# Four joints between the stages of a two-block transformer kernel: order of a projection loop, loads of a gate matrix and of expert rows, and the way sums are read back

## The chip, the cores and the metric

The kernel runs on one core of one Trainium2 chip. The metric is device time in microseconds (us). Before the change the median of 3 runs is 3617.73 us (3616.99 to 3620.08). The profiled execution took 3617.26 us; its span from the first to the last instruction is 3615.6 us, so 1.7 us lie around the span.

## The reference, cut to what matters

Two blocks are computed on 1024 tokens of width 1024, in float32. Each ends in a mixture of experts (32 experts, top 2; then 64 experts, top 8), computed in blocks of 128 slots.

```python
def first_block(x, ...):
    u = rms_norm(h, norm_mix_g)
    x_rnn, g_rnn, q_c, kv_c, k_pe, gate_logits = split(u @ w_in)
    ya = rg_lru(causal_conv(x_rnn)) * gelu(g_rnn)
    yb = mla(q_c, kv_c, k_pe, ...)          # low-rank q and kv, 16 heads, chunk-causal attention
    gates = sigmoid(gate_logits)            # [2, D]
    h = h + (gates[0] * ya + gates[1] * yb) @ w_out
    h = h + hier_moe(rms_norm(h), ...)      # 32 experts, top 2
    return h

def second_block(x, ...):
    mix = hybrid_mixer(h)                   # HGRN2 in four heads, and multiscale_pool, then w_out
    h = layer_norm(ALPHA * h + mix)
    h = layer_norm(ALPHA * h + moe_ffn(h))  # 64 experts, top 8, and one shared expert
    return h
```

In a mixture each token's row goes to its experts' blocks, `silu(x @ w_gate[e]) * (x @ w_up[e]) @ w_down[e]` is taken there, weighted, and added to the token's sum.

## The kernel before, in words

The kernel is a row of stages, each a function with its own block of instruction streams for TensorE (PE), VectorE (DVE), ScalarE (ACT), GpSimd (POOL) and SyncE (SP). A stage ends in a barrier of all engines: the next one starts when the last engine's stream is through. `T` = 8 token tiles of 128 rows, `C` = 8 chunks of 128 columns. In order:

- `begin`, `lru` (the recurrent branch, four blocks of 256 columns; POOL writes zeroes into the spare rows and into the second half of `token_sums`; at its end PE computes the low-rank projection of token tile 0, `low_rank`).
- `mla_project`: for each tile t, `turn_low(t)` transposes the normalized low-rank rows on PE (8 transposes, L662), `low_groups(t + 1)` multiplies the next tile's (L653), `up_groups(t)` multiplies the transposed rows, after DVE has taken them from PSUM (L804), with `w_uq` and `w_ukv` (L679), and between the two it calls `turn_heads(t - 1)` (L692). ACT takes each product; four PSUM banks turn in the order of the list `order`. The two matrices are loaded by SP at the stage's start (L629, L630).
- `attention`, whose SP stream loads the heads two pairs ahead.
- `merge`: the gates (L1133) with `w_gate` loaded in four quarters into two buffers (L1102), then `w_out`, and the rows for the experts are written to DRAM.
- `route1`: DVE picks the experts; SP asks for the weights of the first `W1` = 5 experts, three transfers of 1 MB each (L1626, L1631).
- `dispatch`: DVE computes masks, counts and slots; SP writes the weights by row (`dense`, L1454) into the same DRAM rows; the last DVE instruction (L1614) leaves the token of every slot in `G.slot_tok`. It is used for both mixtures. In the second one the shared expert's products stand in it too, until after the slots are known.
- `experts`: per block of 128 slots POOL gathers the rows (`gather`: index copy L1753, an addition L1756 that makes the index visible, indirect DMA L1757), PE transposes them (`turn_rows`, L1814), DVE copies them out (L1911 for the first, L1902), DVE copies the second half's expert weights into a staging buffer (`stage_gate_up`, L1888, one copy of 128x4096), PE multiplies (L1825, L1828, L1851, L1854), and POOL adds the result into `token_sums` in DRAM. A weight slot is loaded again when PE is through with it (the waits on `gu_ready`).
- `take_sums`: the sums lie in two halves of `token_sums`. SP reads the first half's eight row tiles (L1247); POOL adds the second half to each by an accumulating DMA when the first has landed (`add_second`, L1230); PE transposes (L1260), DVE copies (L1267).
- `hgrn`, `pooling` (SP asks for `w`, `w_pool`, `w_out` at L2273 to L2275; POOL clears the second half of the sums again with nine DMAs of 512 KB, L276), `mix_out`, `route2`, `dispatch`, `experts` for the second mixture (two of four weight slots are loaded before it, and SP asks for the other two at its start), `final_norm` (SP reads the sums, L2481, POOL adds the second half as above, ACT and DVE normalize each tile, SP writes it out).

```python
            for t in range(T):                    # mla_project, PE
                turn_low(t)
                if t + 1 < T:
                    low_groups(t + 1)
                up_groups(t)
            turn_heads(T - 1)
...
            v.wait_ge(x_turned, 1)                # experts, DVE, before its loop
            d.tensor_copy(x_t[:, 0], x_ps[:]).then_inc(x_ready, 1)
            stage_gate_up(0, 0)
            stage_gate_up(1, 1)
```

Of the kernel before, what the change touches and what calls it, by code (L numbers as in the profile page):

```python
# [18 lines left out]
F32 = mybir.dt.float32  # L19
# [6 lines left out]
P = 128  # L26
# [246 lines left out]
def zero_second(pool, sum_d, zero, zero_out):  # L273

    for t in range(T + 1):
        pool.dma_start(sum_d[S + P + t * P:S + P + (t + 1) * P, :], zero).then_inc(zero_out, 16)  # L276


def lru(nc, A, G, spare, sum_d, wcol, wgate, w_low, ps):
# [9 lines left out]
    with ph.ctx:  # L289
# [43 lines left out]
        def _(pool):  # L333
# [6 lines left out]
            zero_second(pool, sum_d, zero[:, 0:D], zero_out)  # L340
            pool.wait_ge(zero_out, 16 * (len(spare) + T + 1))
# [234 lines left out]
def mla_project(nc, A, G, qk_d, v_d, w_low, ps):  # L576
# [12 lines left out]
    with ph.ctx:  # L589
# [54 lines left out]
        def _(pe):  # L644
# [198 lines left out]
def attention(nc, A, G, qk_d, v_d, mask_d):  # L843
# [25 lines left out]
    with ph.ctx:  # L869
# [42 lines left out]
        def _(sp):  # L912
# [20 lines left out]
            for p in range(PAIRS - 2):  # L933
                reload(p)

# [125 lines left out]
def merge(nc, A, G, rows_d, sum_d, logits):  # L1061
# [5 lines left out]
    COL = 2 * D + Q_LORA + KV_LORA + ROPE + D  # L1067
    HC = C // 2
    with ph.ctx:
        w_gate = ph.sb("w_gate", [P, 2, C, D // 4])  # L1070
# [17 lines left out]
        (wg0, wg1, wo_in, x_in, g_ready, g_taken, m_ready, o_ready, o_taken, dve) = ph.sems(  # L1088
            "wg0 wg1 wo_in x_in g_ready g_taken m_ready o_ready o_taken dve")
        wg = [wg0, wg1]  # L1090
# [5 lines left out]
        def _(sp):  # L1096
            w = A["w_in"].rearrange("l (c p) n -> p (l c) n", p=P)
# [129 lines left out]
def add_second(pool, sum_d, rows, row_in, both_in):  # L1227
    for t in range(T):
        pool.wait_ge(row_in[t], 16)
        pool.dma_start(rows[:, t, :], sum_d[S + P + t * P:S + P + (t + 1) * P, :],  # L1230
                       accum_op=ALU.add).then_inc(both_in[t], 16)


def take_sums(nc, G, sum_d, rows, cols):

    ph = phase(nc)
    with ph.ctx:
        tp = ph.ps("tp", [P, 2, C, P])
        turned, taken = ph.sems("turned taken")
        row_in = ph.sems(" ".join(f"row_in{t}" for t in range(T)))  # L1240
        both_in = ph.sems(" ".join(f"both_in{t}" for t in range(T)))
# [7 lines left out]
        @block.gpsimd  # L1249
        def _(pool):  # L1250
            add_second(pool, sum_d, rows, row_in, both_in)

        @block.tensor
        def _(pe):
            for t in range(T):
                pe.wait_ge(both_in[t], 16)
# [7 lines left out]
        def _(v):  # L1264
            for t in range(T):
                v.wait_ge(turned, t + 1)
# [1443 lines left out]
```

## Time and profile before

| what | value |
|---|---|
| median of 3 runs | 3617.73 us |
| profiled execution | 3617.26 us, span 3615.6 us |
| PE busy | 3229.3 us, 89% of the span |
| DVE, ACT, POOL busy | 43%, 20%, 20% |
| PE's longest waits at joints | `take_sums` 29.4 us, `dispatch` (first) 23.8, `pooling` 19.6, `mla_project` 16.8, second `experts` 15.1 and 4.0, `merge` 8.9 |

How to read it: PE is the engine that works through nearly all of the span. What it waits for stands mostly at the joints, where a stage has just ended in a barrier and the next one's data are still on their way. A row of the timeline says when an instruction (or a run of alike ones) began, how long it took, its engine, line and tiles, and in brackets how long its engine had stood idle before it and what ended that. "PEq" and "POOLq" as a releaser are the sequencers, which is what a barrier looks like. SPq and ACTq rows are DMA issues.

### The profile page before, as it was taken

How to read it: one execution, taken by the hardware profiler on the slowest of the kernel's cores; microseconds unless marked ns; L12 is line 12 of the kernel's file. 1: busy time of each engine (PE TensorE's matmuls, PEld its weight loads, DVE VectorE, ACT ScalarE, POOL GpSimd, SP SyncE). 2: the span in 40 equal slices, each digit the busy share in tenths (PEclk: the TensorE clock that was granted, in tenths of full speed). 3: DMA queues.
4: the chain of work that ended last, by engine and by line, in shares of the span. 5: the costliest groups of instructions: out<-in, count | busy, mean ns of one | idle time of the engine just before them, and what ended most of it. 6: DMA issues, size and time to landing. Idle time of an engine off the chain costs nothing. (4 is left out here: it accounts for less than half of the span.)

```text
span 3615.6 us, 44557 instructions
## 1 busy us (share of the span) xinstructions
PE 3229.3 (89%) x14147; PEld 1611.6 (45%) x14148; DVE 1567.9 (43%) x2350; ACT 727.6 (20%) x1169; POOL 728.1 (20%) x932
## 2 busy tenths in 40 slices
PE   8999899978998995989688996999799999999992
PEld 4444355535664453333266773455333333333330
DVE  3332224446773123434346664334344444444444
ACT  2222223334552000111022220121011111111112
POOL 1000000000000000434410000000255555555552
PEclk9999999998999995999789998999899999999996
DMA  6110021123212215999530003101598999888876
GB/s 220 41 41 29 8 97 47 47 64 84 60 48 82 77 66 209 340 384 384 175 84 23 23 0 125 65 31 73 210 310 284 308 327 335 282 278 278 282 246 181
DMA packets 177201, 564.75 MB, mean 156 GB/s; under 512 B 18636, under 2 KB 88880, under 8 KB 139952
## 3 DMA queue, kind: packets, MB, share of 16 engines
q1 hardware_dynamic: 139456, 428.64, 31.3%
q0 software_dynamic: 35856, 133.74, 15.1%
q10 hardware_dynamic: 1800, 1.20, 0.1%
q8 instruction: 54, 0.88, 0.1%
q14 instruction: 35, 0.29, 0.0%
HBM read 460.27 MB, written 103.27 MB: 156 GB/s over the span
## 5 line engine op out<-in xcount | busy, mean ns | idle before, releaser
L1825 PE MATMUL gu_ps<-w_gu,second 128*64 x1680 | 755.4, 603 | 13.3 <-DVE h L1888 8.0
L1828 PE MATMUL gu_ps<-h,second 128*64 128x512 f32 x1680 | 755.4, 603 | 0.0
L1825 PEld LDWEIGHTS gu_ps<-w_gu,second 128*64 128x64 f32 x1680 | 224.3, 138 | 456.0 <-issue 444.2
L1753 POOL COPY idx<-moe_slot_tok 128x1 int32 (+1 forms) x109 | 21.9, 201 | 1782.4 <-POOLq L95 1739.8
L1851 PE MATMUL y_ps<-w_dn,hid_t 128*64 x824 | 375.6, 598 | 0.4 <-issue 0.2
L1854 PE MATMUL y_ps<-second,hid_t 128*64 128x512 f32 x824 | 375.7, 599 | 0.0
L352 PE MATMUL front<-second,wcol 128*128 128x512 f32 x768 | 330.4, 593 | 4.8 <-ACTq L63 2.4
L1888 DVE COPY h<-w_gu 128x4096 f32 x109 | 249.7, 2292 | 70.8 <-SPq L1705 70.5
L352 PEld LDWEIGHTS front<-second,wcol 128*128 128x128 f32 x768 | 145.9, 190 | 188.4 <-issue 188.4
L1773 POOL TENSOR_TENSOR idx_y<-moe_slot_tok,moe_side 128x1 int32<-128x1 int32 x103 | 123.2, 1196 | 520.4 <-ACT second L1874 520.4
L1828 PEld LDWEIGHTS gu_ps<-h,second 128*64 128x64 f32 x1680 | 224.3, 138 | 0.0
L1874 ACT ACTIVATE second<-y_ps,share 128x1024 f32<-128x1024 f32 x103 | 114.6, 1113 | 457.1 <-PE y_ps L1854 457.1
L1868 ACT ACTIVATE act_g<-gu_ps 128x256 f32<-128x256 f32 x105 | 40.2, 383 | 749.7 <-PE gu_ps L1828 749.7
L1851 PEld LDWEIGHTS y_ps<-w_dn,hid_t 128*64 128x64 f32 x824 | 104.3, 136 | 189.4 <-issue 177.5
L1777 POOL TENSOR_TENSOR mark_y<-tok 128x1 f32<-128x1 f32 x103 | 180.7, 1755 | 19.7 <-DMA token_sums<-second,idx_y 9.0
L1778 POOL DMA_INDIRECT token_sums<-second,idx_y x103 | 174.8, 1697 | 18.4 <-issue 17.5
L1900 DVE TENSOR_TENSOR hid<-act_g,gu_ps 128x256 f32<-128x256 f32 x105 | 44.2, 421 | 291.9 <-ACT act_g L1868 291.9
L1904 DVE COPY hid_t<-h_ps 128x256 f32<-128x256 f32 x105 | 44.5, 424 | 277.1 <-PE h_ps L1837 277.1
L1814 PEld LDWEIGHTS x_ps<-ident,xb 128*128 128x128 f32 x856 | 105.0, 194 | 108.8 <-issue 74.6
L1895 DVE COPY second<-w_dn 128x2048 f32 x105 | 129.0, 1229 | 47.1 <-issue 46.9
L1814 PE MATMUL x_ps<-ident,xb 128*128 128x128 f32 x856 | 125.8, 291 | 22.4 <-DMA xb<-token_rows,idx 22.4
L1902 DVE COPY second<-x_ps 128x1024 f32<-128x1024 f32 x105 | 128.6, 1224 | 24.7 <-PE x_ps L1814 24.7
(435 smaller groups left out, 4902.6 us busy)
## 6 DMA issues: line engine op xcount, KB each, us to landing
w_gu<-in_w_gate_dram SPq DMA_DIRECT2D x96, 1024.0 KB, 13.2
w_gu<-in_w_up_dram SPq DMA_DIRECT2D x96, 1024.0 KB, 17.3
w_dn<-in_w_down_dram SPq DMA_DIRECT2D x96, 1024.0 KB, 10.5
wcol<-in_w_in_dram SPq DMA_DIRECT2D x12, 1024.0 KB, 5.3
qk_by_head<-stage SPq DMA_DIRECT2D x32, 384.0 KB, 3.3
qk<-qk_by_head SPq DMA_DIRECT2D x16, 768.0 KB
token_sums<-zero POOLq DMA_DIRECT2D x19, 512.0 KB, 12.7
token_sums<-second SPq DMA_DIRECT2D x16, 512.0 KB, 2.6
```

Of the source, the lines that this page charges most:

```text
L352: last = nc.tensor.matmul(ps[:, slot, c, h * BANK:(h + 1) * BANK], wcol[:, k, kc, c * P:(c + 1) * P], G.u[:, kc, h * BANK:(h + 1) * BANK], ...
L1773: g.tensor_tensor(idx_y[:, slot:slot + 1], G.slot_tok[:, bass.ds(b, 1)], G.side, ALU.add).then_inc(idx_y_ready, 1)
L1777: g.tensor_tensor(mark_y[:, slot:slot + 1], G.tok[:, 0:1], G.tok[:, 0:1], ALU.add).then_inc(idx_y_ready, 1)
L1778: g.indirect_dma_start(sum_d, bass.IndirectOffsetOnAxis(ap=idx_y[:, slot:slot + 1], axis=0), y[:, slot, :], None, compute_op=ALU.add).then ...
L1814: last = nc.tensor.transpose(x_ps[:, c, :], xb[:, slot, c:D:C], G.ident[:])
L1825: nc.tensor.matmul(gu_ps[0:PART, slot], x_t[:, slot, c, 0:PART], w_gu[:, bass.ds(ws, 1), :, c, :].rearrange("p o g n -> p (o g) n"), start ...
L1828: last = nc.tensor.matmul(gu_ps[PART:P, slot], x_t[:, slot, c, PART:P], st_gu[:, slot, :, c, :], start=c == 0, stop=c == C - 1)
L1851: nc.tensor.matmul(y_ps[0:PART, cs], hid_t[:, slot, c, 0:PART], w_dn[:, bass.ds(ws, 1), c, cs].rearrange("p o n -> p (o n)"), start=c == 0 ...
L1854: last = nc.tensor.matmul(y_ps[PART:P, cs], hid_t[:, slot, c, PART:P], st_dn[:, c, cs], start=c == 0, stop=c == FC - 1)
L1888: d.tensor_copy(st_gu[:, slot].rearrange("p g c n -> p (g c n)"), w_gu[:, bass.ds(e % W, 1)].rearrange("p o g c n -> p (o g c n)")).then_i ...
L1895: d.tensor_copy(st_dn.rearrange("p c n -> p (c n)"), w_dn[:, bass.ds(e % W, 1)].rearrange("p o c n -> p (o c n)")).then_inc(d_staged, 1)
L1902: d.tensor_copy(x_t[:, 1 - slot], x_ps[:]).then_inc(x_ready, 1)
```

## The change

Each edit is at a joint:

1. `mla_project`: the order on PE is `low_groups(t + 1)`, `turn_low(t)`, `up_groups(t)`.
2. `merge`'s first two gate quarters are asked for by SP at the end of `attention`'s stream (`load_gate`), into a buffer that both stages share.
3. `route1` asks for 2 experts' weights (`W_EARLY`), `dispatch` for the other 3, before it waits for `dense`. Large temporaries of the first `dispatch` lie in `G.u` for room.
4. `dispatch` has a POOL stream: when the slots are known and `dense` has landed, it gathers the rows of blocks 0 and 1. `experts` begins without these gathers. In `experts` DVE stages block 0's second-half weights ahead of its wait for the transposed rows.
5. `take_sums`: ACT's queue reads the second half of the sums into a buffer `other`, DVE adds. No accumulating DMA.
6. `final_norm`: the same for tiles 0 and 1; tiles 2 to 7 keep the accumulating DMA.
7. `token_sums` has three parts; the third, for the second mixture, is cleared in `lru` (after its first block) and no longer in `pooling`.

```diff
 mla_project, tensor:
             for t in range(T):
-                turn_low(t)
                 if t + 1 < T:
                     low_groups(t + 1)
+                turn_low(t)
                 up_groups(t)
 lru, gpsimd:
-            zero_second(pool, sum_d, zero[:, 0:D], zero_out)
-            pool.wait_ge(zero_out, 16 * (len(spare) + T + 1))
+            zero_second(pool, sum_d, 1, zero[:, 0:D], zero_out)
+            pool.wait_ge(block_done, 2)
+            zero_second(pool, sum_d, 2, zero[:, 0:D], zero_out)
+            pool.wait_ge(zero_out, 16 * (len(spare) + 2 * (T + 1)))
 attention, sync, at its end:
+            for q in range(2):
+                load_gate(sp, A, G, w_gate, q)
+def load_gate(sp, A, G, w_gate, q):
+    c0 = 2 * D + Q_LORA + KV_LORA + ROPE + D + q * (D // 4)
+    w = A["w_in"].rearrange("l (c p) n -> p (l c) n", p=P)
+    sp.dma_start(w_gate[:, q % 2], w[:, :, c0:c0 + D // 4]).then_inc(G.gate_in[q % 2], 16)
 merge, sync:
             for q in range(Q):
                 if q >= 2:
                     sp.wait_ge(g_ready, (q - 1) * PERQ)
-                c0 = COL + q * (D // Q)
-                sp.dma_start(w_gate[:, q % 2], w[:, :, c0:c0 + D // Q]).then_inc(wg[q % 2], 16)
+                    load_gate(sp, A, G, w_gate, q)
 take_sums:
-        @block.gpsimd
-        def _(pool):
-            add_second(pool, sum_d, rows, row_in, both_in)
+        @block.scalar
+        def _(a):
+            for t in range(T):
+                at = S + P + t * P
+                a.dma_start(other[:, t, :], sum_d[at:at + P, :]).then_inc(row_in[t], 16)
...
+            for t in range(T):
+                v.wait_ge(row_in[t], 32)
+                d.tensor_tensor(rows[:, t, :], rows[:, t, :], other[:, t, :], ALU.add).then_inc(added, 1)
+                if t:
+                    take(t - 1)
+            take(T - 1)
 route1, sync:
-            for e in range(W1):
+            for e in range(W_EARLY):
                 load_expert(sp, G, e, e)
 dispatch:
         @block.sync
         def _(sp):
+            if scores is None:
+                for e in range(W_EARLY, W1):
+                    load_expert(sp, G, e, e)
             sp.wait_ge(dense_ready, 1)
...
+        @block.gpsimd
+        def _(pool):
+            g = nc.gpsimd
+            pool.wait_ge(slots_ready, 1)
+            for b in range(2):
+                g.tensor_copy(G.idx[:, b:b + 1], G.slot_tok[:, b:b + 1]).then_inc(idx_ready, 1)
+            pool.wait_ge(idx_ready, 2)
+            pool.wait_ge(dense_out, 16)
+            g.tensor_tensor(G.mark[:], G.tok[:, 0:2], G.tok[:, 0:2], ALU.add).then_inc(idx_ready, 1)
+            for b in range(2):
+                g.indirect_dma_start(G.xb[:, b, :], None, rows_d, bass.IndirectOffsetOnAxis(
+                    ap=G.idx[:, b:b + 1], axis=0)).then_inc(G.xb_in[b], 16)
 experts, gpsimd:
-            gather(0, 0)
-            gather(1, 1)
 experts, vector:
+            stage_gate_up(0, 0)
             v.wait_ge(x_turned, 1)
             d.tensor_copy(x_t[:, 0], x_ps[:]).then_inc(x_ready, 1)
-            stage_gate_up(0, 0)
             stage_gate_up(1, 1)
 pooling:
-        @block.gpsimd
-        def _(pool):
-            nc.gpsimd.memset(zero[:], 0.0).then_inc(cleared, 1)
-            pool.wait_ge(cleared, 1)
-            zero_second(pool, sum_d, zero[:], zero_out)
-            pool.wait_ge(zero_out, 16 * (T + 1))
 final_norm (FIRST = 2):
-            add_second(pool, sum_d, G.h, row_in, both_in)
+            add_second(pool, sum_d, 2, FIRST, G.h, row_in, both_in)
...
+            for t in range(FIRST):
+                at = 2 * (S + P) + t * P
+                a.dma_start(other[:, t, :], sum_d[at:at + P, :]).then_inc(other_in[t], 16)
...
+            for t in range(FIRST):
+                v.wait_ge(row_in[t], 16)
+                v.wait_ge(other_in[t], 16)
+                d.tensor_tensor(G.h[:, t, :], G.h[:, t, :], other[:, t, :], ALU.add).then_inc(both_in[t], 1)
```

## Rows read from the trace of the kernel before

**Rows 1.** The page's engine row: busy us, share, instructions.
```profile
PE 3229.3 (89%) x14147; PEld 1611.6 (45%) x14148; DVE 1567.9 (43%) x2350; ACT 727.6 (20%) x1169; POOL 728.1 (20%) x932
```

**Rows 2.** Timeline, ACT at the start of the projection: start, us, instruction, [idle <-releaser].
```profile
448.48 0.87 ACT L721 ACTIVATE low<-front 128x384 f32<-128x384 f32 x2 [12.80 <-PEq L696]
```

**Rows 3.** DMA view: issues, KB each, median us from issue to landing.
```profile
w_ukv<-in_w_ukv_dram SPq DMA_DIRECT2D x1, 2048.0 KB, 18.5
...
second<-in_x_dram SPq DMA_DIRECT2D x1, 4096.0 KB, 14.1
...
token_rows<-dense SPq DMA_DIRECT2D x1, 128.0 KB, 22.0
```

**Rows 4.** Timeline, PE in the projection: first, middle and last tile.
```profile
454.59 15.21 PE L653 MATMUL front<-w_low,second 128*128 128x384 f32 x48
469.64 15.61 PE L679 MATMUL front<-w_uq,low_t 128*128 128x512 f32 x36
...
581.75 1.04 PE L662 MATMUL front<-ident,low 128*128 128x128 f32 x8
...
625.86 1.04 PE L662 MATMUL front<-ident,low 128*128 128x128 f32 x8
...
758.31 1.04 PE L662 MATMUL front<-ident,low 128*128 128x128 f32 x8
...
760.67 15.72 PE L679 MATMUL front<-w_uq,low_t 128*128 128x512 f32 x36 [1.32 <-DVE low_t L804]
```

**Rows 5.** Windows: busy us of PE, PEld, DVE, ACT, POOL; PEclk, DMA share, GB/s.
```profile
755.00:790.00 35.00, 31.12 (x101) 15.04 (x99) 18.55 (x25) 14.03 (x30) 0.00 (x0) 1.00 0.22 61
...
1475.00:1720.00 245.00, 228.88 (x1072) 84.83 (x1068) 103.83 (x111) 28.07 (x37) 107.18 (x146) 0.97 1.02 381
...
1125.00:1130.00 5.00, 5.00 (x8) 2.15 (x9) 0.00 (x0) 0.00 (x0) 0.00 (x0) 0.63 1.04 404
```

**Rows 6.** Timeline, the joint of attention and merge.
```profile
1117.68 1.02 SPq L1102 DMA_DIRECT2D w_gate<-in_w_in_dram  x2
...
1124.73 35.70 PE L1133 MATMUL ps<-second,w_gate 128*128 128x512 f32 x78 [8.87 <-DMA w_gate<-in_w_in_dram]
```

**Rows 7.** Timeline, from the first route through dispatch into experts.
```profile
1401.57 0.17 DVE L1507 TENSOR_SCALAR tok<-tok 128x8 f32<-128x8 f32 x1 [6.73 <-PEq L95]
...
1404.40 0.38 SPq L1454 DMA_DIRECT2D token_rows<-dense  x1
...
1430.55 1.05 POOL L1757 DMA_INDIRECT xb<-token_rows,idx  x1 [0.37 <-issue]
...
1435.02 1.97 PE L1814 MATMUL x_ps<-ident,xb 128*128 128x128 f32 x8 [6.81 <-DMA xb<-token_rows,idx]
...
1441.01 1.11 PE L1825 MATMUL gu_ps<-w_gu,second 128*64 x1 [4.02 <-DVE h L1888]
```

**Rows 8.** Timeline, the first reading of the sums, first issue and last transposes.
```profile
1789.10 3.98 SPq L1247 DMA_DIRECT2D second<-token_sums  x8
...
1822.62 1.09 PE L1260 MATMUL tp<-ident,second 128*128 128x128 f32 x8 [0.68 <-DMA second<-token_sums]
```

**Rows 9.** Timeline, the start of pooling.
```profile
2203.76 0.38 SPq L2273 DMA_DIRECT2D w<-in_w_in_dram  x1
...
2221.24 14.25 PE L2296 MATMUL u_ps<-h,w 128*128 128x512 f32 x29 [19.62 <-DMA w_pool<-in_w_pool_dram]
```

**Rows 10.** Timeline, the start of the second experts stage.
```profile
2561.76 0.18 POOL L1753 COPY idx<-moe_slot_tok 128x1 int32<-128x1 int32 x1 [351.93 <-POOLq L95]
...
2564.31 0.47 SPq L1631 DMA_DIRECT2D w_dn<-in_w_down_dram  x1
...
2577.75 1.11 PE L1825 MATMUL gu_ps<-w_gu,second 128*64 x1 [4.00 <-DVE h L1888]
```

**Rows 11.** Timeline, ACT in the last stage, first and last of eight tiles.
```profile
3577.91 1.06 ACT L2501 ACTIVATE junk<-second 128x1024 f32<-128x1024 f32 x1 [28.70 <-DMA second<-token_sums]
...
3604.26 1.06 ACT L2501 ACTIVATE junk<-second 128x1024 f32<-128x1024 f32 x1 [1.11 <-DMA second<-token_sums]
```

More of the change, by code:

```diff
@@ L840, in _, with attention @@
             norm_heads(T - 1)
-def attention(nc, A, G, qk_d, v_d, mask_d):
+def attention(nc, A, G, qk_d, v_d, mask_d, w_gate):
     ph = phase(nc)
@@ L1224, in _, with add_second @@
             d.tensor_copy(logits, lps)
-def add_second(pool, sum_d, rows, row_in, both_in):
-    for t in range(T):
+def add_second(pool, sum_d, n, first, rows, row_in, both_in):
+    for t in range(first, T):
+        at = n * (S + P) + t * P
         pool.wait_ge(row_in[t], 16)
-        pool.dma_start(rows[:, t, :], sum_d[S + P + t * P:S + P + (t + 1) * P, :],
-                       accum_op=ALU.add).then_inc(both_in[t], 16)
+        pool.dma_start(rows[:, t, :], sum_d[at:at + P, :], accum_op=ALU.add).then_inc(both_in[t], 16)
 def take_sums(nc, G, sum_d, rows, cols):
@@ L1237, in take_sums @@
     with ph.ctx:
+        other = ph.sb("other", [P, T, D])
         tp = ph.ps("tp", [P, 2, C, P])
-        turned, taken = ph.sems("turned taken")
+        turned, taken, added = ph.sems("turned taken added")
         row_in = ph.sems(" ".join(f"row_in{t}" for t in range(T)))
-        both_in = ph.sems(" ".join(f"both_in{t}" for t in range(T)))
         block = ph.ctx.enter_context(nc.Block())
@@ L1406, in shared_add, with dispatch, room @@
                                    op0=ALU.mult, op1=ALU.add).then_inc(G.sh_added, 1)
-def dispatch(nc, G, K, E, NB, rows_d, sum_d, scores=None):
+def dispatch(nc, G, K, E, NB, rows_d, sum_d, n, scores=None):
     ph = phase(nc)
     with ph.ctx:
-        m = ph.sb("m", [P, T, E])[:] if scores is None else G.m
-        before = ph.sb("before", [P, T + 1, E])
-        dense = ph.sb("dense", [P, T, E])
+        taken = [0]
+        def room(name, n):
+            if scores is not None:
+                return ph.sb(name, [P, n])[:]
+            taken[0] += n
+            return G.u[:].rearrange("p c s -> p (c s)")[:, taken[0] - n:taken[0]]
+        m = room("m", T * E).rearrange("p (t e) -> p t e", e=E) if scores is None else G.m
+        before = room("before", (T + 1) * E).rearrange("p (t e) -> p t e", e=E)
+        dense = room("dense", T * E).rearrange("p (t e) -> p t e", e=E)
         cnt = ph.sb("cnt", [P, E])
@@ L1928, in moe_state @@
     G.first = sb(f"moe_first{E}", [1, E], I32)[:]
+    G.xb = sb(f"moe_xb{E}", [P, 2, D + E])
+    G.idx = sb(f"moe_idx{E}", [P, 2], I32)
+    G.mark = sb(f"moe_mark{E}", [P, 2])
+    G.xb_in = [nc.alloc_semaphore(f"xb_in{i}_{E}") for i in range(2)]
     G.used = sb(f"moe_used{E}", [1, 1], I32)[:]
@@ L2239, in _, with pooling @@
             take_out(H - 1, H)
-def pooling(nc, A, G, sum_d, w_out):
+def pooling(nc, A, G, w_out):
     ph = phase(nc)
@@ L2469, in final_norm @@
         junk = ph.sb("junk", [P, 2, D])
+        other = ph.sb("other", [P, FIRST, D])
         total = ph.sb("total", [P, T])
@@ L2475, in final_norm @@
         both_in = ph.sems(" ".join(f"both_in{t}" for t in range(T)))
+        other_in = ph.sems(" ".join(f"other_in{t}" for t in range(FIRST)))
         block = ph.ctx.enter_context(nc.Block())
@@ L2658, in program @@
                 G.x2 = second[:]
-                attention(nc, A, G, qk_d, v_d, mask_d)
-                merge(nc, A, G, rows1_d, sum_d, logits[:])
+                G.gate_in = [nc.alloc_semaphore(f"gate_in{i}") for i in range(2)]
+                with nc.sbuf_tensor("w_gate", [P, 2, C, D // 4], F32) as w_gate:
+                    attention(nc, A, G, qk_d, v_d, mask_d, w_gate)
+                    merge(nc, A, G, rows1_d, sum_d, logits[:], w_gate)
             G.w_gu = moe.enter_context(nc.sbuf_tensor("w_gu_1", [P, W1, 2, C, F_EXP], F32))
```

68 lines of the change are left out of this document (33 added, 35 removed).

## The prediction

> **What bounds the kernel now.** I read the page's engine row first, then the list of PE's waits, then the timeline around each joint that the diff touches, and last the windows (granted clock and DMA share) for the stretches beside them. PE is busy 89% of the span [rows 1]. So an edit pays by what PE waits at a joint, if the new wait behind it is shorter, and a delay of PE inside a stage is paid in full. Each joint is followed by stages that run at PE's pace, or at that of loads which PE's progress releases, so a joint's gain moves everything behind it. The sum is made against the profiled 3617.26 us, 0.5 us below the median of the runs.
>
> **1. Projection order.** The eye goes to the idle time ahead of the first transposes, 16.8 us. But the stage only opens after its barrier: ACT is released at 448.48 by PE's sequencer [rows 2], so the second tile's products can start at about 448.5 and not at 436. They take 454.59 to 469.64 = 15.05 us, the slow start of the clock included [rows 4], so they end at 463.5. The transposes of tile 0 and the wait for DVE's copy take 760.67 - 758.31 = 2.36 us, as in the last tile, which has no product between the two (rows 4), or 3.3 us if they are still slow: 465.9 to 466.8. The product behind them also waits for w_ukv, asked for at 448.7 and landing 18.5 us later, at 467.2 [rows 3]. So it starts at 467.3 in place of 469.64: a gain of 2.3 us.
> What it costs stands in every later tile. Before, `low_groups` lay between the transposes and the product that needs them, and hid DVE's copy. After, the copy is bare, as in tile 7: 1.32 us of idle, and 0.15 us of overlap lost, 1.47 us. Six tiles (1 to 6) pay it: 8.8 us on a period of 44.11 us (581.75 to 625.86, rows 4). ACT and DVE also do their work later relative to PE: behind tile 7's transposes ACT's square roots for the heads come 6.3 us later, then it takes the low-rank product (0.5 us), and PE needs that bank 7.5 us after the transposes began, so it holds by 0.7 us. The heads' transposes were served in time in tile 7. I add nothing; bound 0 to 0.7 us per tile. This part: +6.5 us (bounds +4 to +11).
> The clock is the open item. Tile 7 has this sequence already, and the window around it has a granted clock of 1.00, the 2.4 GHz level [rows 5], while around 528 us, where PE waited for the heads' copies, it was at the 1.2 GHz level for a few us, at some 1.5 us of loss. By the row I add nothing. The Trainium skill, "TensorE: Matmul & The Clock Gate", section "Part 4: PE-mode transpose", says that a transpose does not count as busy for the gate; an order that puts transposes beside a wait would then fall to the lower level. The result of that is a rival below.
>
> **2. Gates asked for in attention.** PE passes the barrier with SP at 1117.68 and starts at 1124.73, when the quarter lands [rows 6]. SP's stream in attention is idle from 1048.7 on, so 2 MB land there long before 1115. Gain 7.05 us. The lower clock of 1125 to 1130 (0.63, rows 5) costs 3.7 us at half speed, 1.85 us, after 8.9 us of idle; with 1.9 us of idle it may or may not fall. I take 1.0 of 0 to 1.85. This part: -8.0.
>
> **3. Route and first dispatch.** DVE had nothing to do from 1394.84 to 1401.57 [rows 7]: the barrier waited for SP, whose fifteen issues were held up by their own backlog until 1400.7. With six issues (done at 1388) the barrier comes 0.75 us after DVE, and dispatch starts 6.0 us earlier. SP now issues nine loads in dispatch ahead of `dense`; `dense` still lands behind 15 MB on the same queue, at 1404.40 + 22.0 = 1426.4 [rows 3, 7]. So the slots are ready at 1423, POOL waits for `dense` (that is late next), and the gather starts at about 1427.1 instead of 1430.55. It lands 4.45 us later (1430.55 to 1435.0), at 1431.5; the barrier waits for POOL's second issue (about 1 us each), 1430. DVE stages in 1430.0 to 1432.3 under the landing and the transposes (1.97 us), its copy takes 1.25 us, and PE starts at 1434.8 in place of 1441.01. This part: -6.2 (bounds -4.5, if SP's nine issues delay `dense`, to -8.5, if `dense` lands early).
> The stage behind is bound by loads: DMA share 1.02 from 1475 to 1720 [rows 5]. Yet a slot is asked for again only when PE is through with it (first at 1450.7, the moment ACT has the first product), and DMA stood still before that, so the whole stream moves with the start. The third rival takes the opposite.
>
> **4. Sums of the first mixture.** Before: 1789.10 to 1822.6 for 8 reads and 8 accumulating DMAs [rows 8], with DMA saturated. After: 16 plain reads of 512 KB. From the load of x (8 such in 14.1 us) they need at most 28.2 us, from w_uq and w_ukv (6.8 MB in 18.9 us, rows 3) at least 23 us; I take 25.4, last landing 1814.5. Behind it an addition on DVE (1.22 us as its other 128x1024 operations), transposes at the low clock (1.97) and a copy (1.22) against the 1.09 and 1.23 of before: the end at 1819.2 in place of 1825.0. This part: -5.8 (bounds -3 to -7.5). The Trainium skill, "DMA: Bandwidth & Descriptors", section "Issuing engines are not separate DMA queues", speaks against a gain from a second queue: all run on the same 16 engines. The trace agrees, since the engines are full with either; what is saved here is the accumulation's longer time, by the rows.
>
> **5. Pooling.** PE starts at 2221.24 when w_pool has landed [rows 9]. In front of it lie 2.36 MB, and 4.7 MB of zeroes shared the engines. Alone it takes 2203.76, 2 us until data flow (the DMA share is near nothing until 2205.5), and 2.36 MB at 285 GB/s (2 KB packets of 115 ns on 16 engines) to 410 GB/s: 2211.5 to 2214; I take 2213.7. This part: -7.5 (bounds -6.5 to -9.5). The nine clearing DMAs go to `lru`, where DMA is a tenth busy and each weight block is asked for a block (some 95 us) ahead: 0. If that cover were gone, their 12.7 us would show.
>
> **6. Second dispatch and experts.** The slots are known at 2516, the stage begins at 2561.76 [rows 10], so both gathers lie under the shared expert. PE turns the rows at once. DVE stages block 0 when SP says that the weights are in, and SP first issues six loads, until 2564.8; the copy takes 2.29 us, the copy of the rows 1.22: PE starts at 2568.5 in place of 2577.75. This part: -9.2 (bounds -8 to -12, the latter if the clock doesn't fall).
>
> **7. Last stage.** Tiles land every (3604.26 - 3577.91) / 7 = 3.76 us [rows 11]. Two accumulations (2.5 to 3.8 us) turn into two plain reads (1.4 to 1.8 us); these delay the others' start. This part: -1.8 (bounds +0.5 to -4.5).
>
> **Sum:** +6.5 - 8.0 - 6.2 - 5.8 - 7.5 - 9.2 - 1.8 = -32.0; 3617.26 - 32.0 = 3585.3 us.
>
> **The rivals.**
> - The clock falls in the projection. At the one place where it did, the loss was 1.5 us; once in each of seven tiles it is 10.5 us: 3595.8 us. For it: each tile gets a second idle stretch near transposes. Against: tile 7's clock.
> - The order is a gain, as the first idle stretch invites one to think: only the 2.3 us, no cost per tile: 3617.3 - 2.3 - 38.5 = 3576.5. Against: the 1.32 us of tile 7.
> - The first mixture's end is set by its loads and not by its start: the 6.2 us are given back, 3591.5. For it the share of 1.02; against it the idle DMA before the first reload.
> - Slower than before: the same fall of the clock, but lasting. To outweigh the 38.5 us of the other parts by over 7.2 us the projection must lose 45.7 us in seven tiles, 6.5 us each, that is 13 us of each period of 45.6 at the low level. At 4.5 us each the gain is down to 0.2%; there it begins to decide. The longest low stretch seen inside this stage is far shorter.
>
> **How the numbers follow.** The forecast has a chance of 0.72, the clock rival 0.12, the loads rival 0.08, the order-is-a-gain rival 0.04, the slower one 0.01; 0.03 is left for no change (several joints give back). A range of 3576 to 3597 takes in the first, the two rivals behind it and the bounds of the parts, which are largely independent (all at one end: 3570 and 3601). About 0.2% (7.2 us) is what a measurement of this kernel can tell from no change: faster 0.96, same 0.03, slower 0.01.
>
> **What would show it.** Right: PE's first product in merge within 1 us of the barrier; 45.6 us between transposes in the projection, with 1.3 us idle behind each and first product of tile 0 at 467; DVE in dispatch 0.75 us after its last in route; POOL waiting for `dense` and not for slots; pooling's PE at 10 us behind SP; the second experts' PE at 6.8 us behind the barrier. Wrong: granted clock below 1 in the middle of the projection, PE waiting for ACT's bank there, `dense` landing late behind the nine loads, or the first experts stage longer by as much as its start is earlier.

## The result, and the profile after

The changed kernel takes 3591.07 us (median of 4 runs, 3585.51 to 3594.17) against 3618.09 us (median of 4, 3616.99 to 3620.08): a ratio of 0.9923, 95% interval 0.9906 to 0.9940, 27.0 us less. The forecast was 3585.3 us in a range of 3576 to 3597, and faster. The profiled execution, 3585.51 us with a span of 3583.8 us, is the shortest of the four, so its agreement with 3585.3 us says little; the single joints say more. The new order of the projection costs 14.8 us there and not 6.5, and the rest gains more than was forecast, in other proportions.

The page's engine row of the kernel after (compare [rows 1]): PE is busy for 7.8 us more, in the same number of instructions.

```profile
PE 3237.1 (90%) x14147; PEld 1613.8 (45%) x14148; DVE 1577.8 (44%) x2360; ACT 726.0 (20%) x1169; POOL 711.3 (20%) x919
```

**Projection.** Timeline of PE in the kernel after: the first tile, one middle tile, and the last.

```profile
450.14 17.25 PE L656 MATMUL front<-w_low,second 128*128 128x384 f32 x48 [12.49 <-PEq L95]
...
469.79 5.39 PE L682 MATMUL front<-w_uq,low_t 128*128 128x512 f32 x12 [1.52 <-ACT low L724]
...
556.12 15.72 PE L682 MATMUL front<-w_uq,low_t 128*128 128x512 f32 x36 [1.32 <-DVE low_t L807]
571.68 1.04 PE L695 MATMUL front<-ident,qk 128*96 128x128 f32 x8
572.97 1.12 PE L695 MATMUL front<-ident,qk 128*96 128x128 f32 x8 [0.25 <-ACT stage L765]
574.38 1.05 PE L695 MATMUL front<-ident,qk 128*96 128x128 f32 x8 [0.29 <-ACT stage L765]
577.42 1.13 PE L695 MATMUL front<-ident,qk 128*96 128x128 f32 x8 [1.99 <-ACT stage L765]
578.38 8.73 PE L682 MATMUL front<-w_ukv,low_t 128*128 128x512 f32 x16
...
603.50 2.84 PE L682 MATMUL front<-w_uq,low_t 128*128 128x512 f32 x6 [1.32 <-DVE low_t L807]
...
625.74 7.04 PE L682 MATMUL front<-w_ukv,low_t 128*128 128x512 f32 x16
...
777.09 8.42 PE L682 MATMUL front<-w_uq,low_t 128*128 128x512 f32 x19 [1.32 <-DVE low_t L807]
```

The 1.32 us of idle are there in each tile, as forecast. But the product with `w_ukv` takes 8.73 us at 578.38 and 7.04 us at 625.74, the same 16 instructions: 1.69 us lost where the clock is low. The period from 556.12 to 603.50 is 47.38 us; forecast were 45.6. The last tile's product starts at 777.09, 16.42 us later than in [rows 4]; 1.64 us of that came in with the stage before (ACT is released at 450.12, against 448.48 in [rows 2]), in which the clock was low for a moment in this execution. Windows of the same kernel, one tile each (busy us of PE, PEld, DVE, ACT, POOL; granted clock, DMA share, GB/s):

```profile
560.00:606.00 46.00, 42.15 (x138) 23.04 (x137) 16.49 (x26) 14.66 (x33) 0.00 (x0) 0.96 0.16 46
606.00:652.00 46.00, 42.17 (x142) 23.08 (x141) 18.14 (x29) 14.64 (x33) 0.00 (x0) 1.00 0.16 46
652.00:698.00 46.00, 42.18 (x139) 23.27 (x138) 16.54 (x27) 14.64 (x32) 0.00 (x0) 0.96 0.16 46
698.00:744.00 46.00, 42.16 (x139) 22.99 (x138) 16.42 (x29) 14.76 (x33) 0.00 (x0) 0.96 0.16 46
```

Of the first six tiles with heads' transposes, five (those around 531 and 767 included) have a granted clock of 0.96 and one has 1.00; the seventh, behind the last low-rank transposes, is at full clock too. Before, one of the seven had a low stretch.

**First merge**, timeline: PE starts with SP, no longer 7.05 us behind it [rows 6].

```profile
1133.61 0.37 SPq L1112 DMA_DIRECT2D w_out<-in_w_out_dram  x1
...
1133.66 2.81 PE L1141 MATMUL ps<-second,w_gate 128*128 128x512 f32 x6 [1.46 <-PEq L95]
```

**First dispatch**, timeline of the joint of [rows 7]:

```profile
1402.36 0.17 DVE L1552 TENSOR_SCALAR tok<-tok 128x8 f32<-128x8 f32 x1 [0.75 <-PEq L95]
...
1408.11 2.75 SPq L1486 DMA_DIRECT2D token_rows<-h  x1
...
1429.81 0.30 POOL L1500 COPY moe_idx<-moe_slot_tok 128x1 int32<-128x1 int32 x2 [1268.28 <-DVEq L1435]
1433.38 0.19 POOL L1503 TENSOR_TENSOR moe_mark<-tok 128x2 f32<-128x2 f32 x1 [3.27 <-DMA token_rows<-h]
...
1435.49 0.95 POOL L1505 DMA_INDIRECT moe_xb<-token_rows,moe_idx  x1 [0.31 <-issue]
1441.57 1.94 PE L1856 MATMUL x_ps<-ident,moe_xb 128*128 128x128 f32 x8 [12.55 <-PEq L95]
...
1446.33 1.11 PE L1867 MATMUL gu_ps<-w_gu,second 128*64 x1 [2.82 <-DVE second L1954]
```

DVE starts 0.75 us behind its last instruction in route, and POOL waits for the dense weights and not for the slots: both as forecast. But the dense weights land at 1433.4, as far from the first load as before (the 6 us gained in route are lost on the queue), and the barrier opens at 1441.5, 5.1 us after POOL's last issue is through, where the forecast had it open with that issue. The transposes were then waiting for the barrier (PEq) and not for the gather.

**Sums, pooling, second experts, last stage**, timelines of one joint each (rows 8 to 11 are their counterparts):

```profile
1789.21 3.95 SPq L1256 DMA_DIRECT2D second<-token_sums  x8
...
1811.99 1.23 DVE L1284 TENSOR_TENSOR second<-second,other 128x1024 f32<-128x1024 f32 x1
...
1817.06 3.64 SPq L2038 DMA_DIRECT2D w<-in_w_in_dram  x4
...
2194.78 0.38 SPq L2311 DMA_DIRECT2D w<-in_w_in_dram  x1
...
2203.53 11.76 PE L2334 MATMUL u_ps<-h,w 128*128 128x512 f32 x23 [10.88 <-DMA w_pool<-in_w_pool_dram]
...
2541.57 0.33 SPq L1671 DMA_DIRECT2D w_gu<-in_w_gate_dram  x1
...
2549.01 1.11 PE L1867 MATMUL gu_ps<-w_gu,second 128*64 x1 [5.30 <-DVE second L1954]
...
3540.78 1.06 ACT L2545 ACTIVATE junk<-second 128x1024 f32<-128x1024 f32 x1 [19.91 <-DVE second L2571]
...
3572.49 1.06 ACT L2545 ACTIVATE junk<-second 128x1024 f32<-128x1024 f32 x1 [1.14 <-DMA second<-token_sums]
```

Each is read as a distance between SP's first issue in the stage and the first work behind it. Sums: SP to the next stage's SP 27.85 us, 36.68 before (1789.10 to 1825.78). Pooling: 8.75 us, 17.48 before. Second experts: 7.44 us, 16.02 before (SP at 2561.73). Last stage, from SP's first read to the end of the span: 3583.8 - 3534.76 = 49.04 us, 52.06 before.

### The profile page after: what moved, and what is told of

The parts are those of the page before. It is cut to its first block and busy times, and to the rows that moved or that the text cites. A ratio compares the mean times of both kernels' runs of the same rounds, so it can differ in the third digit from the quotient of the medians.

```text
span 3583.8 us, 44567 instructions
## 1 busy us (share of the span) xinstructions
PE 3237.1 (90%) x14147; PEld 1613.8 (45%) x14148; DVE 1577.8 (44%) x2360; ACT 726.0 (20%) x1169; POOL 711.3 (20%) x919
## 5 line engine op out<-in xcount | busy, mean ns | idle before, releaser
L1856 PEld LDWEIGHTS x_ps<-ident,moe_xb 128*128 128x128 f32 x856 | 104.5, 193 | 104.9 <-issue 93.1
L1856 PE MATMUL x_ps<-ident,moe_xb 128*128 128x128 f32 x856 | 125.1, 290 | 18.7 <-PEq L95 17.5
```

The costliest lines, as they stand in the source:

```text
L1856: last = nc.tensor.transpose(x_ps[:, c, :], xb[:, slot, c:D:C], G.ident[:])
```

## The experiments

Twelve runs, each beside runs of the kernel before, whose medians lie between 3617.5 and 3618.4 us. "Changed kernel" is the one above, 3591.1 us; `again` is a second measurement of it, and where a difference to the changed kernel is given below, it is taken from the mean of the two medians, 3591.4. Periods, starts and landings are read from one profiled execution of each kernel.

**The changed kernel again.**

> The changed kernel once more, in the same rounds as the three beside it, for a clock count of its own. If the five low stretches of the clock in the projection belong to the new order, at least four of its tile periods are again near 47.3 us and at most three near 45.7 us, and the median lies near 3590 us. If they were chance, most periods are 45.7 us and the median lies near 3585 us.

3591.65 us, ratio 0.9927 (0.9912 to 0.9941). The tile periods, read from DVE's copies of the turned rows, were 47.4, 47.4, 45.7, 47.3 and 47.3 us. The low clock belongs to the order. It stays at one place: it begins as the heads' transposes end, and the products with `w_ukv` behind them take 8.2 to 8.7 us instead of 7.03.

**The former order, and the new order alone.** In `old_order` the former loop is put back into the changed kernel (shown below); `order_alone` makes the reverse edit, and that alone, in the kernel before.

```
 for t in range(T):
+    turn_low(t)
     if t + 1 < T:
         low_groups(t + 1)
-    turn_low(t)
     up_groups(t)
```

> The changed kernel with the projection's former order in all tiles (transposes of a tile, then the next tile's low-rank products), all else as changed. Theory A, idle time and a lower clock in each tile: the projection's period is 44.1 us again, the merge starts some 14 us earlier, the time is 13 to 16 us below that of the changed kernel. Theory B, only the 1.3 us of idle is due to the order and the clock's dips are chance: 6 to 8 us below. Theory C, given back at a later load: 0 to 3 us below.

3576.12 us, ratio 0.9889 (0.9874 to 0.9903): 15.2 us below the changed kernel. Its clock isn't free of low stretches either: three of its seven tiles have one, the last of them in tile 7. Timeline of this kernel:

```profile
783.97 8.59 PE L682 MATMUL front<-w_ukv,low_t 128*128 128x512 f32 x16
```

> The kernel before with the new order of the projection alone. Theory A (idle and clock in each tile): 12 to 16 us slower than before, with a period of 47.3 us in most tiles. Theory B (idle alone): 6 to 8 us slower, periods of 45.7 us.

3631.73 us, ratio 1.0034 (1.0020 to 1.0047), 13.9 us slower. Periods of 47.3, 47.4, 47.4, 45.7 and 47.3 us. The two runs agree with each other and with theory A, and the medians show nothing of the loss given back.

**What lowers the clock: the wait behind the low-rank transposes, or the heads' transposes?** Three kernels with products that add nothing to the result (PE writes them to a bank that is overwritten next). `filled_wait` has three of them behind the low-rank transposes, in the wait of 1.32 us; `longer_tile` has the former order and two of them in each tile; `heads_filled` has the new order and two of them in the wait of 1.97 us among the heads' transposes:

```
 def turn_heads(t):
     for n in range(TURNS):
+        if n == TURNS - 2 and t + 1 < T:
+            m = number["up", t + 1, NQ]
+            pe.wait_ge(acc_taken, m - 3)
+            for i in range(2):
+                matmul(acc[:, m % 4, :], G.u[:, 0, 0:P], G.u[:, i, 0:BANK], start=True, stop=True)
```

> The changed kernel with three more products of 128x512 on PE between a tile's transposes and its up products, written to a bank that is overwritten next: they add no result, they fill the 1.3 us in which PE waits for DVE's copy. Theory A1, the waiting beside the transposes lowers the clock: no tile period is above 46.0 us, and the time is 5 to 8 us below that of the changed kernel. Theory A2, the transposes lower it whatever stands behind them: the periods stay at 47.3 us, the time is that of the changed kernel within 2 us.

3597.5 us, ratio 0.9940 (0.9927 to 0.9953), by the median 6 us slower than the changed kernel (the intervals overlap), which neither theory had. It is my error of size: such a product is two records of 0.43 us, so three take 2.6 us and not 1.3, and a tile at full clock lasts 46.7 us instead of 45.7, some 8 us in eight tiles. The periods were 46.7, 48.3, 46.7, 48.4 and 48.3 us: three still with the loss, and the last tile's product with `w_ukv` (8.73 us) has it too. With PE busy where it had waited, the clock still falls.

> The changed kernel with the projection's former order, and two products of 128x512 (0.86 us each, 1.72 us) added behind each tile's low-rank products, to a bank that is overwritten next. PE waits nowhere more than in the former order; only the tile is longer, 45.8 us in place of 44.1. In all traces so far the clock's low stretch begins as the heads' transposes end, not at those of the low-rank rows. Theory P, it depends on the time at which the heads' transposes come: three or more of the periods from the second tile on carry a further 1.5 us (47.3 us), and the kernel is 17 to 24 us slower than with the former order alone. Theory W, the bare wait behind the low-rank transposes lowers the clock: at most two periods are long, and it is 13.8 us slower (8 times 1.72), 16 at most.

3597.07 us, ratio 0.9941 (0.9926 to 0.9957), 21.0 us slower than `old_order`: theory P. Here PE has products to do behind the low-rank transposes of every tile, and all six periods are 47.3 to 47.6 us (six of seven tiles with a low stretch, three in `old_order`). One of its tiles in the windows:

```profile
548.00:595.00 47.00, 44.48 (x144) 24.56 (x143) 17.35 (x29) 14.86 (x33) 0.00 (x0) 0.96 0.16 45
```

> The changed kernel, new order of the projection included, with two products of 128x512 (1.72 us) put into the wait of 1.97 us ahead of a tile's last heads' transposes, to a bank that is overwritten next. A tile should take no longer by them. Theory H, the waiting among the heads' transposes makes the clock fall behind them: no low stretch from the second tile to the last, periods of 45.7 us, 5 to 8 us below the changed kernel (3591.4). Theory L, the low-rank transposes with the bare wait make it fall: four or more periods of 47.3 us, the time within 2 us of the changed kernel.

3586.07 us, ratio 0.9913 (0.9898 to 0.9928), 5.3 us below the changed kernel. The intervals overlap, so what decides for theory H is the trace. One of its tiles in the windows, and the timeline of the next one:

```profile
560.00:606.00 46.00, 43.90 (x146) 23.77 (x145) 18.03 (x29) 14.87 (x36) 0.00 (x0) 1.00 0.16 46
```

```profile
619.17 1.88 PE L692 MATMUL front<-second 128*128 128x512 f32 x4
621.32 1.13 PE L700 MATMUL front<-ident,qk 128*96 128x128 f32 x8 [0.26 <-ACT stage L770]
622.28 7.08 PE L682 MATMUL front<-w_ukv,low_t 128*128 128x512 f32 x16
...
645.75 4.56 PE L682 MATMUL front<-w_uq,low_t 128*128 128x512 f32 x10 [1.32 <-DVE low_t L812]
```

The bare wait of 1.32 us is still there, and the clock is 1.00 in every tile; the products behind the heads take 7.03 to 7.14 us. The periods are 45.7 us, but for the first (46.7, with a new wait of 0.70 us for ACT). So in this loop the fall needs the wait among the heads' transposes, and the low-rank transposes with their own wait don't cause it.

**Low-rank transposes in that wait.** The products that fill it can be useful ones. `early_turn` and `turn_in_wait` keep the former order of the products and call the next tile's `turn_low` inside `turn_heads`, at n = 7 and at n = 6:

```
+turn_low(0)
 for t in range(T):
-    if t + 1 < T: low_groups(t + 1)
-    turn_low(t)
-    up_groups(t)
+    if t + 1 < T: low_groups(t + 1)
+    up_groups(t)             # at k == NQ: turn_heads(t - 1, t + 1); for t == 0: turn_low(1)
...
 def turn_heads(t, low=T):
     for n in range(TURNS):
+        if n == TURNS - 2 and low < T:      # early_turn: TURNS - 1
+            turn_low(low)
```

> The changed kernel with a third order in the projection: the low-rank transposes of the next tile are put into the wait of 1.97 us that PE has ahead of the last heads' transposes of a tile, and the next low-rank products stay ahead of the up products, so DVE's copy has cover. If that wait is set by the store of the stage buffer and not by PE, the transposes (0.87 us of PE) are free in seven tiles: 5 to 7 us below the version with the former order. If the transposes beside the heads' lower the clock in each tile, 3 to 6 us above it.

3579.77 us, ratio 0.9894 (0.9879 to 0.9909), no better than the former order, with periods of 45.2, 44.0, 44.0, 44.4 and 45.2 us: three of its seven tiles have a low stretch, as in `old_order`. The trace shows the transposes behind the wait and not in it: there are eight calls of four transposes, and the wait stands ahead of the seventh.

> As early_turn, but with the next tile's low-rank transposes one pair of heads' transposes earlier, ahead of the wait of 1.97 us instead of behind it (in early_turn they came behind it and the period stayed at 44.0 us). If that wait is set by the store of the stage buffer, the period falls by 0.9 us to 43.1 us, and the time is 5 to 8 us below that of the former order (3576.1), 3568 to 3571 us. If the wait only moves, the period stays at 44.0 us and the time within 2 us of it.

3573.34 us, ratio 0.9880 (0.9865 to 0.9895). Timeline of this kernel:

```profile
613.81 1.04 PE L665 MATMUL front<-ident,low 128*128 128x128 f32 x8
615.97 1.13 PE L699 MATMUL front<-ident,qk 128*96 128x128 f32 x8 [1.12 <-ACT stage L769]
616.93 7.03 PE L684 MATMUL front<-w_ukv,low_t 128*128 128x512 f32 x16
```

The wait shrank from 1.97 to 1.12 us, the periods are 43.2 to 43.3 us but for the first (43.8), no tile has a low clock, and the first merge starts at 1111.15 instead of 1119.87 in `old_order`, whose three low stretches are part of the difference. The medians are only 2.8 us apart, where 5 to 8 were expected, and the intervals overlap. In the profiled executions the 8.7 us are there at the merge and 6 of them are gone in the first mixture; what that can be, the control under `sums_back` shows.

**The joint in front of the first experts.** `gather_in_experts` puts the two gathers back; `dense_first` moves one line group in SP's stream of dispatch:

```
+sp.wait_ge(dense_ready, 1)
+sp.dma_start(rows_d[0:S, D:D + E]..., dense[:])
 if scores is None:
     for e in range(W_EARLY, W1):
         load_expert(sp, G, e, e)
-sp.wait_ge(dense_ready, 1)
-sp.dma_start(rows_d[0:S, D:D + E]..., dense[:])
```

> The changed kernel with the first mixture's two gathers back at the start of experts; nine loads in dispatch, DVE's new order and everything else stay. Theory D, the barrier behind dispatch waits until POOL's gathers have landed: it now opens at the landing of the dense weights, 0.5 us behind it instead of 8, the first block is gathered from there, and the first product on PE comes 2 to 5 us earlier against the start of dispatch (44.0 us in the changed kernel). Theory N, the barrier only waits for what is issued: the gathers come later by the barrier and the product 2 us later. For the time of the whole: if the first mixture's end follows its start, the same sign and size; if its loads set it, within 1.5 us of the changed kernel.

3588.63 us, ratio 0.9918 (0.9905 to 0.9932): 2.7 us below the changed kernel by the medians, which the intervals alone don't separate; the trace does. From DVE's start in dispatch (1401.99) to the first product it is 42.4 us against 44.0; in the eight other kernels with these gathers and loads in dispatch (`again` and `sums_back` among them) it is 44.0 to 45.3. Timeline of this kernel:

```profile
1433.84 0.18 POOL L1798 COPY moe_idx<-moe_slot_tok 128x1 int32<-128x1 int32 x1 [1272.53 <-POOLq L95]
...
1440.83 1.97 PE L1860 MATMUL x_ps<-ident,moe_xb 128*128 128x128 f32 x8 [12.19 <-DMA moe_xb<-token_rows,moe_idx]
...
1444.39 1.11 PE L1871 MATMUL gu_ps<-w_gu,second 128*64 x1 [1.59 <-DVE second L1958]
```

Without the gathers in front of it the barrier opens at 1433.8, with them at 1441.5. Theory D: behind dispatch all engines wait until POOL's gathers have landed. The traces show it directly. POOL's `DRAIN`, the record ahead of its part in the barrier, runs from 1434.38 to 1440.64 in the changed kernel, and the second gather's last landing is at 1440.50; in `dense_first` it ends at 1435.29, with the landing at 1435.15. In `gather_in_experts` the same record takes 0.08 us.

> The changed kernel with the dense weights stored ahead of the nine expert loads in dispatch instead of behind them. Theory Q, the store lands late because of what is queued ahead of it: it lands before the slots are known (27 us behind dispatch's start), the gathers start at once, the first product comes 3 to 4 us earlier against the start of dispatch. The loads then start 2.5 us later. Whole time: 3 us lower if the mixture's end follows its start, 0 to 2.5 us higher if its loads set the end.

3588.13 us, ratio 0.9919 (0.9905 to 0.9932). From DVE's start (1400.49) to the first product it is 40.5 us, 3.5 less, as theory Q has it. Timeline of this kernel:

```profile
1403.32 0.38 SPq L1483 DMA_DIRECT2D token_rows<-h  x1
...
1430.14 0.95 POOL L1505 DMA_INDIRECT moe_xb<-token_rows,moe_idx  x1 [0.31 <-issue]
1436.21 1.94 PE L1856 MATMUL x_ps<-ident,moe_xb 128*128 128x128 f32 x8 [9.07 <-PEq L95]
...
1440.98 1.11 PE L1867 MATMUL gu_ps<-w_gu,second 128*64 x1 [2.82 <-DVE second L1954]
```

POOL no longer waits for the dense weights, and the barrier again opens 5.1 us after its last issue is through (1431.09 to 1436.2). The end of the first mixture follows: 383.1 us from dispatch's start against 386.9, in one execution each. The loads don't give it back.

**The former way of reading the sums.** `take_sums` as before, its second reads accumulating on POOL's queue.

> The changed kernel with the first mixture's sums taken as before, eight reads and eight accumulating reads behind them. In the trace of the changed kernel this joint, from the first read's issue to the first load of the next stage, took 27.9 us against 36.7 us. If that is gained for the whole, it is 8 to 9.5 us slower than the changed kernel (3591.4), about 3600 us. If the next stage gives part of it back, less: 5 us for the predicted size.

3602.25 us, ratio 0.9956 (0.9943 to 0.9970), 10.9 us above the changed kernel. SP to SP 37.2 us against 27.85. Timeline of this kernel:

```profile
1794.89 4.00 SPq L1256 DMA_DIRECT2D second<-token_sums  x8
...
1818.35 0.85 POOL L1240 DMA_DIRECT2D second<-token_sums  x1 [2.99 <-DMA second<-token_sums]
1832.09 3.75 SPq L2027 DMA_DIRECT2D w<-in_w_in_dram  x4
```

The last accumulation is only issued at 1818.35, each of the last four 3.8 us behind the one before, since each waits for the landing of its tile's plain read; with plain reads alone the last addition was under way at 1811.99. In the trace a packet of 4096 bytes takes 159 ns (median) in the plain reads and 328 ns in the accumulating ones. The Trainium skill, "DMA: Bandwidth & Descriptors", section "Issuing engines are not separate DMA queues", says that transfers started from several engines share the same 16 DMA engines. What the second queue was worth here doesn't contradict it: the same bytes are read by the same engines, in packets that take half as long. No run keeps plain reads and makes the second wait for the first, so what the former order of waiting cost by itself isn't shown.

In the ten other kernels with plain reads and additions SP to SP took 27.9 to 29.5 us, and 37.1 in `order_alone`, which has the accumulation: the gain of 8.8 us between the two profiles above stands at the upper end of some 7 to 9.

This run is also a control for the stage ahead of it, in which it is the changed kernel instruction for instruction. Its first product is at 1446.45 (1446.33 in the changed kernel), yet its stage ends at 1794.9 and not at 1789.2. The windows of the two, `sums_back` first and the changed kernel second:

```profile
1700.00:1750.00 50.00, 45.44 (x203) 16.17 (x200) 20.59 (x20) 4.49 (x6) 26.32 (x32) 0.93 0.93 333
```

```profile
1700.00:1750.00 50.00, 48.10 (x232) 18.17 (x230) 21.85 (x24) 5.99 (x8) 21.73 (x32) 1.00 0.90 319
```

In the profiled executions the stage takes either 342.6 to 344.1 us from first product to end (the changed kernel, `again`, `old_order`, `gather_in_experts`, `dense_first`) or 346.9 to 348.7 (all the others, the kernel before among them), and only the long ones have a low stretch of the clock within this window. Between `sums_back` and the changed kernel it goes with the execution and not with an edit. That the 5.2 us by which the stage is longer in the profile before, and the 5.9 us between `turn_in_wait` and `old_order`, are of this kind is the likely reading; no second profile of those kernels shows it.

**All that helped.** `combined` is the changed kernel with `turn_in_wait`, `dense_first` and `gather_in_experts`.

> The changed kernel with the three edits that the runs point to: the next tile's low-rank transposes in the heads' wait (turn_in_wait), the dense weights stored ahead of the nine loads, and the first mixture's gathers in experts. From dispatch's first instruction to the first product: the slots are known after 27.4 us (dense_first), the barrier opens 0.6 us later, from there 10.6 us as in gather_in_experts: 38.6 us, against 44.0 in the changed kernel, 40.5 and 42.4 with either edit alone. If the end follows the start, 5.4 us below turn_in_wait (3573.3): 3567.9 us. If the first mixture's loads take some of it back, 3568 to 3573. Above 3575 one of the edits costs something that its own run hid.

3563.54 us, ratio 0.9850 (0.9833 to 0.9867): 54.7 us below the kernel before and 27.8 below the changed one. Timeline of this kernel:

```profile
1409.18 0.18 POOL L1802 COPY moe_idx<-moe_slot_tok 128x1 int32<-128x1 int32 x1 [1246.82 <-POOLq L95]
...
1416.23 1.97 PE L1864 MATMUL x_ps<-ident,moe_xb 128*128 128x128 f32 x8 [8.58 <-DMA moe_xb<-token_rows,moe_idx]
...
1419.80 1.11 PE L1875 MATMUL gu_ps<-w_gu,second 128*64 x1 [1.59 <-DVE second L1962]
```

Dispatch started at 1381.00, so the first product comes 38.8 us later; 38.6 were expected. The median is 9.8 us below `turn_in_wait`, 4.4 more than expected; the two were measured in separate sets of runs, and no run here says where the rest is from.

## Why the prediction was right, and where it was not

Forecast, and distance measured between the two profiles, in us; the last column says what it is read from.

| part | forecast | measured | read from |
| --- | --- | --- | --- |
| 1 projection order | +6.5 | +14.8 | last tile's product, less 1.64 brought in |
| 2 gates | -8.0 | -9.4 | lateness +16.3 at attention's end, +6.91 at route's SP |
| 3 first dispatch | -6.2 | -1.6 | +6.91 at route's SP, +5.32 at first product |
| 4 sums | -5.8 | -8.8 | SP to SP |
| 5 pooling | -7.5 | -8.7 | SP to first product |
| 6 second experts | -9.2 | -8.6 | SP to first product |
| 7 last stage | -1.8 | -3.0 | SP to the end of the span |
| sum | -32.0 | -25.3 | |

The medians differ by 27.0 us, the profiled executions by 31.8: beside the parts above these hold +1.6 before the projection, -5.2 within the first mixture (likely the low stretch of the control above), and -2.8 elsewhere, 2.5 of it between pooling's first product and the second experts. That the median lies in the range is in part luck, because errors of both signs met: +8.3, +4.6 and +0.6 for parts 1, 3 and 6 against -6.8 for the other four. Parts 1 to 4 each came out beyond the bounds that the prediction had set for them. Its widest sum is off as well: with all parts at their upper ends it is 3599.7 us and not 3601.

- **Part 1** had the exposed copy right and missed the clock. From tile 0's product to tile 7's PE needs 16.3 us more than before: 8.8 are the forecast six times 1.47 us, some 7 are the clock, and 0.5 is left over (a period at full clock is 45.66 us, not 45.58). The step that failed is "By the row I add nothing": tile 7's clock of 1.00 was one sample. In `old_order` the same tile, with the same instructions in the same order, has a low stretch (8.59 us for the product with `w_ukv` that took 7.04 before). What happened is the first rival in price, 1.7 us a tile in five of them against 1.5 in one before, but not in cause. It named a second idle stretch near transposes, while `heads_filled` shows that the wait that counts is the old one among the heads' transposes, and `longer_tile` that with a tile made longer by 1.72 us, without that second stretch, six of seven tiles lose the clock. The rest of the error is the first tile, where 1.5 us were gained and not 2.3. Its low-rank products took 17.1 us to the transposes behind the long idle stretch, where 15.05 were taken, and what PE waited for then was ACT (1.52 us). In `order_alone` the same tile gained 2.1.
- **The rule of the Trainium skill** that was set against the row, "TensorE: Matmul & The Clock Gate", section "Part 4: PE-mode transpose", says that a transpose does not count as busy for the gate. The low-rank transposes beside their bare wait did not lower the clock in any tile of `heads_filled`; the heads' transposes with their waits did in five tiles of the changed kernel, and two ordinary products in their midst (1.88 us) were enough to stop it. The rule fits the second, and alone would have put the fall in the wrong place. It doesn't say either why the same heads' transposes with the same waits kept the full clock in six of seven tiles of the kernel before.
- **Part 2** gained the forecast 7.05 us and the whole of the clock as well, where 1.0 us had been taken: with an idle time of 1.46 us instead of 8.87 the products started at full clock.
- **Part 3** failed at two steps. "`dense` still lands behind 15 MB on the same queue" took the landing of before, 22.0 us behind its issue at 1404.4, but the nine loads that now stand ahead of it started only at 1402.3, so it landed at 1433.4 (`dense_first` removes this: 3.5 us). And "the barrier waits for POOL's second issue (about 1 us each)" was wrong: it waits for the landing (`gather_in_experts`, `dense_first`, and the landings in the traces). The start was 4.6 us worse than forecast. Seen by itself, dispatch lost: from DVE's start to the first product it took 39.4 us before and 44.0 after, and what is left of a gain is the 6.1 us that route became shorter by. `combined`, with both steps undone, takes 38.8. The rival that the mixture's end is set by its loads is refuted by `dense_first`, whose end moved with its start.
- **Part 4** was a size: the sixteen plain reads had landed by 1812.0, 22.8 us behind the first issue, where 25.4 were taken and 23 was the bound. The median of `sums_back`, 10.9 us higher, confirms the gain for the whole time.
- **Parts 5 to 7** were as forecast but for 1.2 us in pooling (its loads landed 8.7 us behind SP, not 10) and in the last stage, and the barrier-hold of part 3 is hidden in the second dispatch by the shared expert (POOL's last issue there is through at 2499.6, 42 us before the next stage). These three were read in the traces alone; no run undid them.

## What to carry to other kernels

A bare wait on PE is priced by its length and by what it does to the clock further on, and the place of the fall isn't the place of the edit: compare the duration of the same products tile by tile, and in more than one execution, before blaming a wait or clearing it, and prefer to fill an existing wait with work that is due anyway (`turn_in_wait`) to shuffling work around it. A gather that is moved ahead of a barrier is not free behind it: here the barrier held all engines until it had landed, so it pays only where other engines have work for that long. A small store that someone waits for goes ahead of the large loads on its queue; and when a profile agrees with a forecast to 0.2 us, check the joints one by one, since a single execution carries several us of clock that belong to no edit.

## What the runs showed of the hardware that was not expected

- The granted clock falls behind the heads' transposes in some tiles and not in others, with the same instructions and the same gaps of 0.25, 0.29 and 1.97 us among them. With tile periods of 44.0 to 44.1 us (at full clock) it fell in one to three of seven tiles (one in the kernel before, three in `old_order` and `early_turn`), with periods of 45.7 us and over in four to six (four in `filled_wait`, five in each of the six kernels with the new order and no products added, six in `longer_tile`). With the 1.97 us wait filled it fell in none (`heads_filled`, `turn_in_wait`, `combined`). No run moved the transposes in time while leaving the period alone, so what of the timing decides is left open.
- POOL's `DRAIN` ahead of the barrier at the end of dispatch lasted until 0.14 us behind the last landing of its gathers, in the changed kernel and in `dense_first`; all engines started 0.9 us later. Without gathers in front of the barrier it opened at 1433.8 (`gather_in_experts`), 0.9 us behind the landing of the dense weights.
- Accumulating reads of 512 KB came every 3.8 us beside plain ones and every 2.5 us once the plain ones were through (`sums_back`), with packets of 328 ns against 159 ns; sixteen plain reads of that size took 22.8 us together, 1.4 us each (some 370 GB/s).
